# The slabs behind an inner norm run on the raw residual; the norm's mean and deviation are applied to their outputs

## The chip, the cores and the metric

The kernel runs on one core of a Trainium2 chip. The metric is the time of one execution on the device, in microseconds (us). The engines are TensorE (PE, with PEld for its weight loads), VectorE (DVE), ScalarE (ACT), GpSimd (POOL) and SyncE (SP, which only issues DMAs here).

## The reference, cut to what matters

Two layers work on 512 latent tokens and 256 context tokens of 1024 features. Layer 0 has attention, layer 1 gated linear attention (GLA); the second half of each layer is a gated ConvFFN. Every half ends in a residual sum and a layer norm, and the next half reads the normed stream, modulated by vectors that come from a conditioning vector:

```
def layer_norm(x, g, b):
    mu = mean(x); var = mean(square(x - mu))
    return (x - mu) * rsqrt(var + EPS) * g + b
sh1, sc1, g1, sh2, sc2, g2 = split(silu(cond) @ ada_w[i] + ada_b[i], 6)
a = h * (1 + sc1) + sh1
y = attn_mixer(a) if i % 2 == 0 else gla_mixer(a)
h = layer_norm(ALPHA * h + g1 * y, ln_g[i, 0], ln_b[i, 0])
u = (h * (1 + sc2) + sh2) @ w_up            # 1024 -> 5632
acc = conv_b + centred depthwise convolution of width 3 over tokens of u
f = (silu(gate half of acc) * value half of acc) @ w_down
h = layer_norm(ALPHA * h + g2 * f, ln_g[i, 1], ln_b[i, 1])
```

So there are four norms. Norm 0 stands between attention and FFN 0, norm 1 between FFN 0 and GLA, norm 2 between GLA and FFN 1 (512 tokens only, as norm 3), and norm 3 makes the output. The first three are the inner norms. Because a norm with modulation is linear in the tokens once mean and deviation are known, W·(gain·(h − mean)·rstd + shift) equals rstd·(W·(gain·h)) − mean·rstd·(W·gain) + W·shift.

## The kernel before

**Slabs.** The stream lies feature-major: `h_res` is 8 tiles (KT) of 128 features by 768 tokens (TOK) in fp32. Weights come as 185 slabs of 128x1024 fp32, each giving 128 output features from 8 input tiles. SP's queue loads them in order into four buffers (`slab_load`, L390); a load waits until the w_lo of four slabs before is made. ACT makes w_hi of a slab (L998, L1011), DVE w_lo = raw − w_hi (`rest`, L1452), and TensorE does for each k-tile hi·hi, hi·lo and lo·hi (`slab` L519 to L535, `slab_high_first` L514). ACT and DVE split slab s+2 while slab s runs. The outputs go to four PSUM tiles pm[0] to pm[3].

**Ada pairs.** The modulation vectors need 48 tiles of `ada_w`, loaded in pairs of 1 MB on the same SP queue (`ada_load`, L395), with `ada_taken` counting the pairs that DVE has reduced; the load of pair n waits for `ada_taken` n−1. DVE reduces a pair (`ada_pair`, four row sums L1476, L1478 and `take_pair` L1482 to L1486, which writes `mods`) in `beside`, behind two of the four slabs of an iteration of FFN 0. Ahead of the FFN 0 loop SP issues slab loads up to S_FFN0+7, `ada_load(22)`, and then the loop with the slab loads S_FFN0+8 and on.

**A norm.** While the last eight slabs before a norm come out, DVE adds the residual (L1657) and its sum over tiles (L1664), ACT squares, POOL adds the squares (`sums_phase`, L2069). `stats` (L600) then turns sums into means per token with matmuls that give 128x6 results, DVE's `norm_phase` (L1705) makes variance and reciprocal on 128x6 tiles, and two sets of matmuls (`spread`) spread mean and reciprocal over partitions into PSUM. DVE subtracts the mean (L1728) and multiplies by the reciprocal (L1734), each with one operand in PSUM. ACT's `modulate` (L1024) applies the fused gain and shift per tile (L1030) and makes x_hi (L1041), and x_lo comes from DVE for tiles 0, 3, 6 and from POOL for the other five (`low_part`, L2051). TensorE works on two slabs at once while the tiles arrive (`first_modulated`, L562 to L594) and then goes on with whole slabs. In GLA the first of them gives the gate's low-rank input, from which `logits` (L818) and `decays` (L1818) go in pairs between the next slabs. `fuse` (L1687) makes gain and shift from `mods`, `ln_g` and `ln_b`.

**FFN.** Up slabs come in groups of 8, 8 and 6 pairs, each followed by 8 down slabs. Of a pair, ACT makes the centre tap (L1170), DVE the two side taps and the product (L1779), and the result is split into hid_hi and hid_lo.

Of the kernel before, what the change touches and what calls it, by code (L numbers as in the profile page):

```python
# [59 lines left out]
PAIR_AFTER = (3, 4, 6, 7, 9, 10, 12, 13, 14)  # L60

# [14 lines left out]
class Order:  # L76
# [14 lines left out]
    def enter(self, i, per):  # L91
        self.extra, self.start, self.per = i * per, self.n, per

    def leave(self, count):
        assert self.n - self.start == self.per, (self.n - self.start, self.per)
        self.n, self.extra = self.start + self.per * count, 0


def trunk(nc, x_in, vec_in, rep_in, slabs_in, gates_in, first_in, ada_in, rope_in, band_in, eye_in, a2_in, level_in, out):
    ctx = ExitStack()  # L100
    with ctx:
# [34 lines left out]
        mean_w = place("mean_w", [1])  # L136
        ones = place("ones", [1])
# [7 lines left out]
        stat_a = place("stat_a", [2, 6])  # L145
# [29 lines left out]
        [mod_t], _ = scratch(free_at + 2 * 4 * TOK, ("mod_t", [4, TOK]))  # L175
# [3 lines left out]
        [gla_v, cum], _ = scratch(hid_at, ("gla_v", [TOK // P, 8 * P]), ("cum", [2, GLA_HEADS, TOK]))  # L179
# [16 lines left out]
        for b in range(3, GLA_LEVELS):  # L196
# [4 lines left out]
        [o_hi2], at = scratch(x_at, ("o_hi2", [KT, LAT]), dtype=FP32R)  # L201
        [pairs, o_g], at = scratch(at, ("pairs", [2, LAT]), ("o_g", [2, LAT]))
        assert at <= x_at + 4 * KT * TOK
        [faded], at = scratch(x_at + 4 * KT * TOK, ("faded", [4, LAT]))
        [o_lo2], at = scratch(at, ("o_lo2", [KT, LAT]), dtype=FP32R)
        assert at <= hid_at
# [12 lines left out]
                 "stat_done", "h_ready", "mod_f", "x_hi_done", "centred", "std_done", "lin_done", "silu_done",  # L219
# [5 lines left out]
                 "var_done", "std2", "less_mean", "mean_done", "rms_done", "spread", "r_done", "squared_h",  # L225
                 "x_sum", "gate_done", "gate_copied", "gate_open", "added", "sink_done", "low_v", "low_p", "ln_scaled", "stat_a", "mean_b", "stat_copied", "key_r"]
# [155 lines left out]
        def _(sp):  # L382
# [68 lines left out]
            with sp.Fori(2, 12) as i:  # L451
                for u in range(4):
                    slab_load(4 * i + u + S_FFN0, u)
                    if u % 2 == 1:
                        ada_load(2 * i + u // 2 + 19, 1 - u // 2)
            for i in range(12, 17):
                for u in range(4):
                    slab_load(4 * i + u + S_FFN0, u)
                    if u % 2 == 1 and 2 * i + u // 2 + 19 < ADA_TILES:
                        ada_load(2 * i + u // 2 + 19, 1 - u // 2)  # L460
# [40 lines left out]
        def _(pe):  # L501
# [60 lines left out]
            def first_modulated(base, c, tokens):  # L562

                lag = 2 if tokens == TOK else 3
                out_of = (lambda slot: pm[slot ^ base % 2]) if base != S_GLA else (lambda slot: pm[slot])
                pe.wait_ge(sem["split_lo"], base + 2)
                pe.wait_ge(sem["psum_free"], base)

                def high(slot, k):
                    for w in (w_hi, w_lo):  # L570
                        for at, a, b in pieces(tokens):
                            pe.matmul(out_of(slot)[:, at:at + b - a], w[slot][:, k * P:(k + 1) * P], x_hi[:, k, a:b],
                                      start=(k == 0 and w is w_hi), stop=False)

                def low(slot, k):
                    for at, a, b in pieces(tokens):
                        last = pe.matmul(out_of(slot)[:, at:at + b - a], w_hi[slot][:, k * P:(k + 1) * P], x_lo[:, k, a:b],
                                         start=False, stop=(k == KT - 1))
                    return last

                one, two = base % 2, (base + 1) % 2
                for k in range(KT):
                    slots = (one, two) if k < KT - lag else (one,)
                    pe.wait_ge(sem["x_hi_done"], KT * (c + 1) + k + 1)
                    for slot in slots:
                        high(slot, k)
                    pe.wait_ge(*low_of(c, k))
                    for slot in slots:
                        last = low(slot, k)
                last.then_inc(sem["slab_done"], 1)  # L590
                for k in range(KT - lag, KT):
                    high(two, k)
                    last = low(two, k)
# [1642 lines left out]
```

## Time and profile before

| | us |
|---|---|
| Median of three runs | 1715.65 |
| Lowest and highest | 1715.63, 1716.13 |
| Span of the profiled execution | 1712.9 |
| PE busy | 1651.3 (96%) |
| PEld busy | 1496.0 (87%) |
| DVE busy | 1103.4 (64%) |
| ACT busy | 711.4 (42%) |
| POOL busy | 100.0 (6%) |

The span is that of the profiled execution; the runs are timed from outside and lie some 2.75 us above it. The span holds 24053 instructions. In rows of the timeline the columns are the start in us, the duration, the engine, the line of the kernel, the operation with its output and inputs, and in brackets the idle time before it and what ended it. Consecutive equal instructions are drawn together as "xN" with one duration from the first's start to the last's end.

### The profile page before, as it was taken

Reading aid. Unit: us, or ns where it says so; the run is one execution under the profiler, and the core shown is the slowest. Engines: PE = TensorE matmul, PEld = TensorE weight load, DVE = VectorE, ACT = ScalarE, POOL = GpSimd, SP = SyncE. Lnnn points to the kernel's source line nnn. Section 1 sums busy time; section 2 is a strip of 40 time slices with the busy share of each in tenths; the row PEclk is TensorE's granted clock in tenths of the full one; section 3 lists DMA queues with packets and bytes.
Section 4 is the critical chain, followed back from the end, with each engine's and each line's share of the span. In section 5 each row is a group of like instructions: output and inputs, shape, how many; then the busy total and the mean of one; then the engine's idle time right before and its main releaser. Section 6 shows DMA issues by size and latency. Waiting matters only on the chain.

```text
span 1712.9 us, 24053 instructions
## 1 busy us (share of the span) xinstructions
PE 1651.3 (96%) x9008; PEld 1496.0 (87%) x9008; DVE 1103.4 (64%) x1796; ACT 711.4 (42%) x1104; POOL 100.0 (6%) x81
## 2 busy tenths in 40 slices
PE   8999999998999999999999899999989999999997
PEld 7999877898999999999999887977777788888885
DVE  6678666476888578865776555166645664464556
ACT  4222565336333233322334664255534543343345
POOL 0200000122000000000002200010002100000002
PEclk9999999999999999999999999999999999999999
DMA  9334100031434333343312022010123133333332
GB/s 362 129 136 161 49 1 1 25 136 38 139 107 147 135 111 130 115 142 141 111 61 89 27 74 62 24 36 26 38 62 98 62 98 98 99 98 99 92 92 74
DMA packets 37280, 159.51 MB, mean 93 GB/s; under 512 B 4145, under 2 KB 4401, under 8 KB 31057
## 3 DMA queue, kind: packets, MB, share of 16 engines
q1 hardware_dynamic: 37202, 158.44, 27.6%
q8 instruction: 52, 0.85, 0.2%
q14 instruction: 26, 0.21, 0.0%
HBM read 156.33 MB, written 2.10 MB: 92 GB/s over the span
## 4 chain that ended last, share of the span: by engine, by line
PE 87%; DVE 5%; ACT 5%; issue 2%; DMA 1%; POOL 0%; SPq 0%; ACTq 0%; DVEq 0%
PE pm L532 59%; PE pm L514 5%; PE pm L765 4%; PE pm L944 3%; PE pm L685 3%; PE pm L552 2%; PE pm L711 2%; PE pm L886 2%; PE pm L698 1%; ACT mod_t L1030 1%; PE pm L869 1%; DMA ada_w<-first_ada 1%; DVE h_res L1728 1%; PE pm L642 1%; PE pm L598 1%
## 5 line engine op out<-in xcount | busy, mean ns | idle before, releaser
L1452 DVE TENSOR_TENSOR w_lo<-raw,w_hi 128x1024 fp32r<-128x1024 f32 x185 | 231.0, 1250 | 341.5 <-ACT w_hi L1011 338.7
L1011 ACT ACTIVATE w_hi<-raw 128x1024 fp32r<-128x1024 f32 x181 | 191.7, 1059 | 601.6 <-PE pm L532 517.6
L532 PE MATMUL pm<-x_hi,w_hi 128*128 128x384 f32 (+1 forms) x1464 | 422.6, 349 | 1.1 <-DVE w_lo L1452 1.1
L532 PE MATMUL pm<-x_hi,w_lo 128*128 128x384 f32 (+1 forms) x1464 | 421.0, 348 | 0.0
L532 PE MATMUL pm<-x_lo,w_hi 128*128 128x384 f32 (+1 forms) x1464 | 421.0, 348 | 0.0
L532 PEld LDWEIGHTS pm<-x_hi,w_hi 128*128 128x128 f32 x1464 | 266.6, 188 | 16.9 <-issue 1.4
L532 PEld LDWEIGHTS pm<-x_hi,w_lo 128*128 128x128 f32 x1464 | 267.2, 188 | 14.2
L532 PEld LDWEIGHTS pm<-x_lo,w_hi 128*128 128x128 f32 x1464 | 267.3, 188 | 14.0
L1478 DVE CUSTOM_DVE_ANT_0 ada_w<-ada_w,cond_rep 128x1024 f32<-128x1024 f32 x80 | 102.6, 1283 | 0.0
L2069 POOL TENSOR_TENSOR sum<-sum,sq_t 128x768 f32<-128x768 f32 (+1 forms) x28 | 46.8, 1672 | 936.7 <-ACT sq_t L1140 936.7
L532 PE MATMUL pm<-hid_hi,w_hi 128*128 128x384 f32 (+1 forms) x330 | 98.8, 353 | 0.2 <-DVE w_lo L1452 0.2
L532 PE MATMUL pm<-hid_lo,w_hi 128*128 128x384 f32 (+1 forms) x330 | 98.7, 353 | 0.0
L532 PE MATMUL pm<-hid_hi,w_lo 128*128 128x384 f32 (+1 forms) x330 | 98.7, 353 | 0.0
L1196 ACT ACTIVATE hid_hi<-hid_f 128x768 f32 (+3 forms) x44 | 32.6, 742 | 131.0 <-DVE hid_f L1791 131.0
L1476 DVE CUSTOM_DVE_ANT_0 junk_f<-ada_w,cond_rep 128x1024 f32<-128x1024 f32 x56 | 68.3, 1220 | 0.0
L1794 DVE TENSOR_TENSOR hid_lo<-hid_f,hid_hi 128x512 f32 (+2 forms) x44 | 36.3, 826 | 44.7 <-ACT hid_hi L1196 44.7
L532 PEld LDWEIGHTS pm<-hid_hi,w_hi 128*128 128x128 f32 x330 | 60.4, 188 | 4.9 <-DVE w_lo L1452 0.7
L532 PEld LDWEIGHTS pm<-hid_hi,w_lo 128*128 128x128 f32 x330 | 60.3, 188 | 4.3
L532 PEld LDWEIGHTS pm<-hid_lo,w_hi 128*128 128x128 f32 x330 | 60.4, 188 | 4.2
L944 PE MATMUL pm<-x_sum,raw 128*128 128x512 f32 x128 | 59.2, 593 | 0.0
L685 PE MATMUL pm<-qkv 128*128 128x256 f32 (+3 forms) x176 | 55.3, 419 | 2.1 <-ACT probs_t L1077 1.3
L711 PE MATMUL pm<-probs_t,v_tok 128*128 128x128 f32 x400 | 54.0, 279 | 1.5 <-DVE x_lo L1587 0.7
(248 smaller groups left out, 2541.0 us busy)
## 6 DMA issues: line engine op xcount, KB each, us to landing
raw<-slabs SPq DMA_DIRECT2D x185, 512.0 KB, 3.6
ada_w<-ada SPq DMA_DIRECT2D x44, 1024.0 KB, 4.9
ada_w<-first_ada SPq DMA_DIRECT2D x4, 1024.0 KB, 18.3
raw<-gates SPq DMA_DIRECT2D x8, 512.0 KB, 3.5
h_res<-x SPq DMA_DIRECT2D x4, 768.0 KB, 16.3
out<-h_res SPq DMA_DIRECT2D x8, 256.0 KB, 2.0
rope<-rope SPq DMA_DIRECT2D x1, 512.0 KB, 22.9
level_f<-level SPq DMA_DIRECT2D x1, 448.0 KB, 3.2
```

The costliest lines, as they stand in the source:

```text
L514: last = pe.matmul(out_p[:, at:at + b - a], w[slot][:, k * P:(k + 1) * P], x[:, k, a:b], start=(k == 0 and w is w_hi and x is hi), stop=(k ...
L532: last = pe.matmul(out_p[:, at:at + b - a], w[slot][:, ks], x[:, k, a:b], start=(k == 0 and w is w_hi and x is hi), stop=(k == tiles - 1 a ...
L685: last = pe.matmul(pm[n % 3][:, at:at + b - a], q, qkv[:, u["k"], a:b], start=True, stop=(u["band"] is None or at > 0))
L711: last = pe.matmul(weighed(n), v_tok[:, t, u["v"] * P:(u["v"] + 1) * P], probs_t[:, n % 2, j * P:(j + 1) * P], start=(j == 0), stop=(j == ...
L765: last = pe.matmul(pm[j][:, at:at + b - a], w[slot][:, ks], x[:, k, a:b], start=(k == 0 and w is w_hi and x is hid_hi), stop=(k == tiles - ...
L944: last = pe.matmul(gate_bank, gate_raw(i)[:, k * P:(k + 1) * P], x_sum[k][:, :], start=(k == 0), stop=(k == KT - 1))
L1011: act.activation(w_hi[nxt % 2][:, :], raw[nxt % 4][:, :], ACT.Copy).then_inc(sem["split_hi"], 1)
L1452: dve.tensor_tensor(w_lo[nxt % 2][:, :], raw[nxt % 4][:, :], w_hi[nxt % 2][:, :].bitcast(FP32), ALU.subtract).then_inc(sem["split_lo"], 1)
L1476: junk_written = order.mark(dve.tensor_tensor_reduce(junk[:, :], w, cond_rep[:, 0, :], 1.0, 0.0, ALU.mult, ALU.add, to[:, half, 0:1]))
L1478: last = dve.tensor_tensor_reduce(w, w, cond_rep[:, 1, :], 1.0, 0.0, ALU.mult, ALU.add, to[:, half, 1:2])
L1794: dve.tensor_tensor(hid_lo[:, bass.ds(2 * i + u // 2, 1), 0:tokens].rearrange("p a b -> p (a b)"), hid_f[:, 0:tokens], hid_hi[:, bass.ds(2 ...
L2069: pool.tensor_tensor(sum2[:, 0:tokens], sum2[:, 0:tokens], sq_t[:, n % 2, 0:tokens], ALU.add).then_inc(sem["summed"], 1)
```

## The change

The first three slabs behind each inner norm become `raw_slabs`. Their input is the residual times the fused gain, split into hi and lo tile by tile while the residual is made (ACT `raw_hi`, DVE `raw_low`), so they need neither mean nor deviation. Two to four extra columns hold the gain and the shift vectors and give W·gain and W·shift. The statistics are four wide matmuls placed behind k-tile 3 of the first raw slab; mean, deviation and reciprocal are now 128x768 tiles in SBUF (`less`, `rstd`). Norming and modulating run beside the raw slabs for slab 3 (`paced_slab`) and all later ones. The raw outputs are finished in `take_raw` (DVE), a ScalarE `z` and a GpSimd `y`. POOL does seven of the eight low parts. ACT's splits of slabs +2, +3, +4 stand inside its modulating loop (SPLIT_AFTER), DVE's inside its scaling loop (REST_AFTER). The first iteration of FFN 0 has no ada pair any more, every later pair comes one iteration later, and the last group of up slabs has one more. GLA's logits follow other slabs. The last norm keeps its place and takes the wide statistics too. ATTN_OUT and GLA_OUT rotate over four banks.

```diff
+N_RAW = 3
+LOGITS_AFTER = {3: (0, 1), 4: (2, 3), 6: (4, 5), 8: (6, 7)}
-LOW_ON_VECTOR = (0, 3, 6)
+LOW_ON_VECTOR = (KT - 1,)
+SPLIT_AFTER = (0, 3, 6)
+REST_AFTER = (2, 5)
+PAIR_AT = [*range(12), *range(16, 20), *range(12, 16), *range(20, ADA_TILES)]
...
             ada_load(22, 0)
-            with sp.Fori(2, 12) as i:
+            for u in range(4):
+                slab_load(S_FFN0 + 8 + u, u)
+            with sp.Fori(3, 12) as i:
                 for u in range(4):
                     slab_load(4 * i + u + S_FFN0, u)
                     if u % 2 == 1:
-                        ada_load(2 * i + u // 2 + 19, 1 - u // 2)
+                        ada_load(2 * i + u // 2 + 17, 1 - u // 2)
...
+            def stats(c, tokens=TOK):                                   # PE
+                for at, a, b in pieces(tokens):
+                    last = pe.matmul(pm[2][:, at:at + b - a], less_w[:, 0:1].to_broadcast([P, P]), sum1[:, a:b], ...)
+                for at, a, b in pieces(tokens):
+                    last = pe.matmul(pm[3][:, at:at + b - a], mean_w[:, 0:1].to_broadcast([P, P]), sum2[:, a:b], ...)
+            def raw_slabs(c, tokens):
+                for u in range(N_RAW):
+                    pe.wait_ge(sem["split_lo"], base + u + 1)
+                    if u == 2:
+                        pe.wait_ge(sem["std2"], c + 1)
+                    for k in range(KT):
+                        if u == 0:
+                            pe.wait_ge(sem["raw_hi"], KT * c + k + 1)
+                            pe.wait_ge(sem["raw_lo"], KT * c + k + 1)
...
+                        if u == 0 and k == 3:
+                            stats(c, tokens)
+            def paced_slab(c, tokens, out_p):
+                pe.wait_ge(sem["split_lo"], s + 1)
+                pe.wait_ge(sem["psum_free"], s - 1 if c == 1 else s - 3)
...
+            raw_slabs(1, TOK)                                           # GLA
+            paced_slab(1, TOK, pm[1])
+            for u in range(N_RAW, 1 + 2 * GLA_HEADS):
+                if u > N_RAW:
+                    slab(S_GLA, 0, u, hid_hi, hid_lo, TOK if u <= GLA_HEADS else LAT)
+                for j in LOGITS_AFTER.get(u, ()):
+                    logits(j)
...
+                act.activation(tile_for(less), bank_of(pm[2], tokens), ACT.Copy)             # ACT norm_phase
+                act.activation(tile_for(rstd), bank_of(pm[2], tokens), ACT.Square)
+                act.activation(rstd[:, 0:tokens], rstd[:, 0:tokens], ACT.Sqrt, bias=col("eps"))
                 for n in range(KT):
                     act.wait_ge(sem["centred"], KT * c + n + 1)
                     modulate(n, c, tokens)
+                    if n in SPLIT_AFTER:
+                        u = SPLIT_AFTER.index(n)
+                        act.wait_ge(sem["slab_done"], base + u + 1)
+                        split(base + u + 2, base + u + 2)
...
+                dve.tensor_tensor(rstd, bank_of(pm[3], tokens), rstd, ALU.subtract)          # DVE norm_phase
+                def centre(n):
+                    dve.tensor_tensor(h_res[:, n, 0:tokens], h_res[:, n, 0:tokens], less[:, 0:tokens], ALU.add)
+                centre(0)
+                centre(1)
+                dve.wait_ge(sem["std2"], c + 1)
+                dve.reciprocal(rstd[:, 0:tokens], rstd[:, 0:tokens])
+                for n in range(KT):
+                    dve.tensor_tensor(h_res[:, n, 0:tokens], h_res[:, n, 0:tokens], rstd[:, 0:tokens], ALU.mult)
+                    if n + 2 < KT:
+                        centre(n + 2)
+                    if c < 3 and n in REST_AFTER:
+                        rest(base + 2 + REST_AFTER.index(n), ...)
+                take_raw(0)
+                take_raw(1)
+                rest(base + 4, base + 4)
...
+                take_raw(2)
+                rest(base + N_RAW + 2, base + N_RAW + 2)
...
-                        if layer == 0 and u % 2 == 1 and (g < 2 or (s0 == S_LAST_UP and i < 2)):
-                            ada_pair(20 + (s0 - S_FFN0) // 2 + u // 2 + 2 * i, ...)
+                        if layer == 0 and u % 2 == 1 and (g < 2 or (s0 == S_LAST_UP and i < 3)):
+                            ada_pair(18 + (s0 - S_FFN0) // 2 + u // 2 + 2 * i, ...)
...
-                        fuse(1)
+                        gain(1)
+                        fuse(1, tokens)
...
+                pool.tensor_tensor(less_r, less, rstd, ALU.mult)                             # POOL low_part
                 for n in LOW_ON_GPSIMD:
                     pool.tensor_tensor(lo[:, n, 0:tokens], mod_ring[n % 4], hi[:, n, 0:tokens], ALU.subtract)
+                for u in range(N_RAW):
+                    pool.wait_ge(sem["scaled"], N_RAW * c + u + 1)
+                    pool.wait_ge(sem["z_done"], N_RAW * c + u + 1)
+                    pool.tensor_tensor(to, raw_scaled(c, u)[:, 0:tokens], to, ALU.add).then_inc(sem["y_done"], 1)
```

## Rows read from the trace of the kernel before

**Rows 1.** The page, chain of work that ended last, share of the span by engine
```profile
PE 87%; DVE 5%; ACT 5%; issue 2%; DMA 1%; POOL 0%; SPq 0%; ACTq 0%; DVEq 0%
```

**Rows 2.** Windows: us, busy (x) PE, PEld, DVE, ACT, POOL, PEclk, DMA, GB/s
```profile
382.35:416.70 34.35, 28.82 (x170) 27.39 (x169) 20.70 (x28) 23.50 (x34) 9.89 (x6) 0.90 0.05 16
416.70:533.20 116.50, 116.50 (x674) 116.50 (x674) 99.98 (x182) 39.63 (x44) 0.00 (x0) 1.00 0.36 123
949.32:983.54 34.22, 28.97 (x170) 27.22 (x169) 21.56 (x30) 23.37 (x34) 9.19 (x5) 0.90 0.06 17
1319.76:1344.91 25.15, 20.16 (x97) 15.37 (x97) 15.41 (x28) 15.51 (x22) 6.88 (x6) 0.93 0.07 22
396.00:398.00 2.00, 2.00 (x8) 2.00 (x8) 1.88 (x3) 1.97 (x4) 0.00 (x0) 0.50 0.00 0
```

**Rows 3.** Timeline of PE in GLA: first logits, and values turned ahead of the third slab
```profile
983.54 2.84 PE L818 MATMUL pm<-low,a 32*128 32x512 f32 x8
...
1064.75 0.82 PE L838 MATMUL pm<-eye,v_turn 128*128 128x128 f32 x6
```

**Rows 4.** Groups by line and form: busy us, mean ns, idle before; DVE reciprocals
```profile
L1617 DVE RECIPROCAL row<-row 128x1 f32<-128x1 f32 x48 | 7.6, 159 | 0.8
...
L1723 DVE RECIPROCAL small<-small 128x6 f32<-128x6 f32 x2 | 0.4, 191 | 0.7 <-ACT small L1157 0.7
L1579 DVE RECIPROCAL head_r<-head_r 128x36 f32<-128x36 f32 x1 | 0.4, 368 | 0.0
```

**Rows 5.** Timeline of DVE and ACT behind norm 0
```profile
399.59 0.95 DVE L1734 TENSOR_TENSOR h_res<-h_res,pm 128x768 f32<-128x768 f32 x1
400.45 0.95 DVE L1728 TENSOR_TENSOR h_res<-h_res,pm 128x768 f32<-128x768 f32 x1
...
400.93 1.29 ACT L1030 ACTIVATE mod_t<-h_res,fused 128x512 f32<-128x512 f32 x2
...
403.01 1.30 ACT L1030 ACTIVATE mod_t<-h_res,fused 128x512 f32<-128x512 f32 x2
...
414.82 1.06 ACT L1011 ACTIVATE w_hi<-raw 128x1024 fp32r<-128x1024 f32 x1 [2.60 <-PE pm L577]
...
415.91 1.23 DVE L1452 TENSOR_TENSOR w_lo<-raw,w_hi 128x1024 fp32r<-128x1024 f32 x1 [4.79 <-ACT w_hi L1011]
...
426.45 1.22 DVE L1476 CUSTOM_DVE_ANT_0 junk_f<-ada_w,cond_rep 128x1024 f32<-128x1024 f32 x1
```

**Rows 6.** Timeline of POOL and DVE where both work at once
```profile
913.21 1.84 POOL L2069 TENSOR_TENSOR sum<-sum,sq_t 128x768 f32<-128x768 f32 x1 [498.43 <-ACT sq_t L1140]
914.05 2.09 DVE L1452 TENSOR_TENSOR w_lo<-raw,w_hi 128x1024 fp32r<-128x1024 f32 x1 [0.93 <-ACT w_hi L1011]
...
964.92 1.83 POOL L2051 TENSOR_TENSOR x_lo<-mod_t,x_hi 128x768 fp32r<-128x768 f32 x1 [15.75 <-ACT x_hi L1041]
965.48 0.95 DVE L1728 TENSOR_TENSOR h_res<-h_res,pm 128x768 f32<-128x768 f32 x1
...
1331.45 1.28 POOL L2051 TENSOR_TENSOR x_lo<-mod_t,x_hi 128x512 fp32r<-128x512 f32 x1 [11.85 <-ACT x_hi L1041]
```

**Rows 7.** DMA issues from 400 to 560: KB each, median us to landing
```profile
raw<-slabs SPq DMA_DIRECT2D x18, 512.0 KB, 4.0
ada_w<-ada SPq DMA_DIRECT2D x9, 1024.0 KB, 4.8
```

**Rows 8.** Waits of SP from 370 to 640: us in total, times, longest
```profile
SPq L395 <- DVE mods L1486: 123.1, 14, 10.4
```

**Rows 9.** Timeline of PE and DVE in the last norm
```profile
1694.94 2.02 PE L608 MATMUL pm<-mean_w,sum 128*128 128x128 f32 x16
...
1701.48 0.68 DVE L1734 TENSOR_TENSOR h_res<-h_res,pm 128x512 f32<-128x512 f32 x1
```

**Rows 10.** Timeline of PE, down slabs of the last group of FFN 0
```profile
911.74 0.51 PE L514 MATMUL pm<-hid_hi,w_hi 128*128 128x384 f32 x2
```

**Rows 11.** Timeline of PE, third slab of ATTN_OUT
```profile
332.35 0.59 PE L514 MATMUL pm<-x_hi,w_hi 128*128 128x384 f32 x2 [1.33 <-ACT tmp L1130]
```

More of the change, by code:

```diff
@@ L575, in low @@
[L575 removed]
+                            pe.matmul(out_p[:, at:at + b - a], w[s % 2][:, ks], hi[:, k, a:b], start=(k == 0 and w is w_hi),
+                                      stop=False)
+                    pe.wait_ge(*low_of(c, k))
                     for at, a, b in pieces(tokens):
[L577 to L579 removed]
@@ L581, in first_modulated @@
[L581 to L593, printed above, removed]
+                        last = pe.matmul(out_p[:, at:at + b - a], w_hi[s % 2][:, ks], lo[:, k, a:b], start=False,
+                                         stop=(k == KT - 1))
@@ L1141, in evacuate @@
                             sem["squared_h"], 1)
-                in_ffn = base not in (S_ATTN_OUT, S_GLA_OUT)
+                        if norm < 3:
+                            if n == 0:
+                                act.wait_ge(sem["gain_done"], norm + 1)
+                            for k, (a, b) in enumerate(kinds(tokens)):
+                                last = act.activation(RAW[norm][0][:, n, a:b], h_res[:, n, a:b], ACT.Copy,
+                                                      scale=fused[:, 0, n, k:k + 1])
+                            last.then_inc(sem["raw_hi"], 1)
                 if norm is not None:
@@ new lines, in ffn @@
+                    if g == 0:
+                        for u in range(4):
+                            evacuate(s0 + u, 0, u, raw_out(2 * layer, u) if u < N_RAW else pm[3], u if u < N_RAW else None)
+                            if u == 1:
+                                act.wait_ge(sem["slab_done"], s0 + 5)
+                                split(s0 + 6, s0 + 6)
+                        for u in range(4):
+                            step(s0, 1, u, evacuate, out=u, ahead=u > 0)
+                    with act.Fori(2 if g == 0 else 0, tiles // 2) as i:
+                        for u in range(4):
@@ new lines, in fuse @@
+                dve.wait_ge(sem["gain_done"], c + 1)
+                nk = len(kinds(tokens))
+                for o in range(2):
+                    at = tokens + nk * o
+                    hi, lo = (x[:, :, at:at + nk] for x in RAW[c])
+                    order.mark(dve.tensor_copy(hi, fused[:, o, :, 0:nk]))
+                    order.wait()
+                    last = dve.tensor_tensor(lo, fused[:, o, :, 0:nk], hi.bitcast(FP32), ALU.subtract)
+                last.then_inc(sem["extra_in"], 1)
@@ new lines, in ffn @@
+                    if g == 0:
+                        for u in range(4):
+                            evacuate(s0 + u, 0, u, raw_out(2 * layer, u) if u < N_RAW else pm[3], u if u < N_RAW else None)
+                            if u == 1:
+                                rest(s0 + 6, s0 + 6)
+                        for u in range(4):
+                            step(s0, 1, u, evacuate, out=u, ahead=u > 0)
+                            beside(1, u)
+                    start = 2 if g == 0 else 0
@@ new lines, in ffn @@
+                    with nullcontext(0) if unrolled else dve.Fori(start, tiles // 2) as i0:
+                        for i in range(tiles // 2) if unrolled else (i0,):
+                            if not unrolled:
+                                order.enter(i, 4 + per, start)
+                            for u in range(4):
+                                step(s0, i, u, evacuate, out=u)
+                                beside(i, u)
+                            if not unrolled:
+                                order.leave(tiles // 2 - start)
```

513 lines of the change are left out of this document (294 added, 219 removed).

## The prediction, as put on record

> **What bounds the kernel now.** I read the page first: its chain of work that ended last is PE for 87% of the span, with DVE and ACT at 5% each [rows 1]. So nearly all of the time is TensorE, and the change can win only where TensorE stands still or runs at a low clock. Cutting the span into windows around the inner norms shows where that is [rows 2]. From the first statistics matmul of norm 0 to the end of its two paced slabs TensorE is busy 28.82 of 34.35 us at a granted clock of 0.90, behind norm 1 28.97 of 34.22 us, behind norm 2 (512 tokens) 20.16 of 25.15 us. In the first of them the granted clock falls to 0.50, the lower of its two levels: 396 to 398 us, with TensorE busy throughout (last line). In the steady part TensorE is busy all 116.50 us: 14 slabs, so a slab of 768 tokens costs 8.32 us, one of 512 two thirds, 5.5. Two slabs would need 16.6 us where norm 0 takes 34.35: about 15 us a norm are the most that can be won. The steady part also shows DVE busy 99.98 of 116.50 us, 7.14 per slab of 8.32: whatever delays DVE is caught up slowly.
>
> Times below are us behind t0, the end of the last slab before the norm (382.35, 949.32, 1319.76).
>
> **Statistics and reciprocal, norm 0.** The new four statistics matmuls stream 1536 fp32 columns, as many as a pair of logits, which takes 2.84 [rows 3]. I take 2.8. Raw slab 0 starts near 0.8, gives four tiles (4.2), then the statistics: they end at 7.8. Slab 0 ends at 12.0, slab 1 at 20.4. DVE's subtraction and ACT's Sqrt, both 128x768 and about 0.9 to 1.3 each with their hand-over, bring the deviation to 11.0. Then comes a 128x768 reciprocal. The trace has it at 159 ns for 1 column, 191 for 6 and 368 for 36 [rows 4], 6.0 ns a column: 4.7 us, and 3.2 for 512 columns. Bounds: the 0.95 of a plain 128x768 tensor_tensor [rows 5] and, by the 6.4 ns a column between 1 and 6, 5.1. I take 4.7, since its own rows grow that way. The Trainium skill ("VectorE: DVE Perf Modes", First, the fixed hardware budget) says that a reciprocal repeats its divide steps 8 times; at that page's 0.96 GHz an estimate of 6.4 us, dearer than the rows say, by which the sum would be some 5.5 us higher.
>
> **Centring and scaling against GpSimd.** So the first centred and scaled tile is due at 15.7. Before, DVE's two operations a tile had one operand in PSUM and were issued every 0.86 [rows 5], with no loss beside a POOL operation: 0.95 at 965.48 while POOL ran from 964.92 to 966.75 [rows 6]. Afterwards `less` and `rstd` lie in SBUF, so both operands do. The one kind of DVE instruction with two SBUF operands that met POOL here is w_lo: 2.09 instead of 1.23 [rows 5, 6], for it starts at 914.05 and ends at 916.14, 1.09 behind the end of POOL's operation at 915.05. It stood still until POOL was done. The Trainium skill ("SBUF — State Buffer", Who interferes with whom) has that as a rule: a DVE instruction with two SBUF inputs and a GpSimd one that reads SBUF exclude each other for the whole instruction, one with a PSUM operand doesn't. Both rows agree with it. So I let every POOL operation of 1.84 (1.28 for 512 tokens, [rows 6]) insert itself whole into the DVE chain. POOL now has 7 low parts (5 before), `less_r` and 3 y's to do in just that stretch.
> Without exclusion: from 15.7 six DVE operations by 0.87 and the 1.23 of w_lo for slab 2 end at 22.1; six more and the next w_lo at 28.5; PE would do slabs 2 and 3 from 22.1 to 38.8. With it, 3 POOL operations come before the first w_lo (27.6) and 6 before the second (39.5): slab 2 runs 27.6 to 36.0, slab 3, which also follows its tiles, ends at 48.8. ACT at 2.08 a tile [rows 5] keeps ahead of that. Four slabs at 48.8 stand against 34.35+16.6=51.0 before: hardly anything won where 12 could be.
>
> **What is late next: an ada pair.** SP issues in order, and `ada_load(22)` stands ahead of slab loads S_FFN0+8 to 11; it waits for ada pair 20 (`ada_taken` 21). Before, DVE took that pair at once behind the norm, after the first up pair; now the first iteration has no pair and it is taken in i=1, behind the y's (50.7), the w_lo of slab 5 (53.6) and the evacuation of six slabs. Six slabs of DVE work are 6×7.14=42.8, less two pairs at 5.0 (four of 1.22 [rows 5] and their sums): 32.8, so 86.4. A pair's load lands 4.8 after its issue, a slab's 4.0 [rows 7]; slab base+8 queues behind the pair's, so between 4.0 and 8.8: I take 5.7, for both share the queues, and 0.4 for the issue. Then w_hi and w_lo take 2.3 [rows 5]: slab base+8 starts at 94.8, before at 34.35+6×8.32=84.3. **+10.5** (bounds: 0 if DVE is 10 us earlier, +13 if the load takes longest). SP waited for pairs 14 times in 370 to 640 us, up to 10.4 [rows 8]: hidden there because slabs were already in; here all four buffers behind it are empty.
>
> **Norm 1.** Same chain, but slab 3 needs bank 1, which comes free with `take_raw(1)`, behind all centring: start 44.3, end 52.7. The first logits were at 34.2 [rows 2, 3], now at 52.7; behind them one slab of 8.32 instead of three. Old stretch to the third value slab (983.54 to 1065.57 [rows 3]) 82.0, less 16.6, plus about 0.9 for decays with less cover: 119.0 against 116.3, **+2.7** (−10.0 without exclusion).
> **Norm 2**, by the same steps with 3.2, 0.6 to 0.7 a DVE operation and 1.28 a POOL operation: w_lo of slab 2 at 19.5, of slab 3 at 28.1, four slabs at 34.8 against 25.15+11.0=36.1; the raw evacuations then hold the next slabs by some 3: **+1.7** (−7.6 without exclusion).
> **Final norm**: nothing runs beside it, so all that is added is open: reciprocal 3.2 for 0.2, wide subtraction, Sqrt and copy, less the narrow spreads. Old first scaled tile 1701.48+0.68, 7.2 behind 1694.94 [rows 9]; new: 10.3 or so; the last is 0.7 later still because the first two centred tiles no longer run ahead: **+3.8** (bounds +1, +5).
> **Last group of FFN 0.** One ada pair more (i<3), `gain`, the fuse with its copies, before the down slabs: old w_lo ended at 916.14 [rows 6], +5.1 for the pair and 0.4: 921.6; PE wants it at 911.74+6.24 (six of eight k-tiles of 8.32) [rows 10], **+3.7** (bounds 0, +5).
> **Smaller parts.** ATTN_OUT with four banks takes away waits as the 1.33 in [rows 11]: **−1.3**. The raw low and high parts stand behind the down slabs: DVE has there two operations of 0.95 and a w_lo of 1.23 a slab [rows 5], some 1.3 more for the low part, and behind three of eight slabs of ATTN_OUT a pair of 5.0. Those come to 9.5 against 8.32, the next ones to 4.5, so they are made up: nothing (bound +2 at the last pair). The two to four extra columns of a raw slab and the swapped buffers move no slab: nothing.
> **Clock.** A stretch with idle of this kind had 0.90 over 34 us [rows 2], 3.4 us of full clock missing, about 2.5 of it while matmuls ran at 0.50. Two such starts come anew (slab base+8 behind 10 us idle, the slab 3 of norm 1 behind 9): **+5.0** (bounds 0, +8).
> Sum: 10.5+2.7+1.7+3.8+3.7−1.3+5.0=**+26.1**. Span 1712.9+26.1=1739.0; the median of the runs (1715.65) lies 2.75 above the profiled span, and what lies around the span does not change, so **1742**, A.
>
> **Rivals.** *B, the late load is hidden* (pair 20 taken 10 us sooner, or slab 8 landing early): −10.5 and one clock start −2.5: 1729. For it: DVE's pace was summed from averages. *E, the reciprocal costs like any wide operation* (0.95): 3.7 less at two norms of 768 and 2.3 at the other two, 12.0: 1730. Against it: three rows on one line. *C, the other side: no exclusion for centring and scaling*, because POOL gets only gaps, or the operations mostly miss each other: 0 in norm 0 (pair 20 taken by 76, just in time), −10.0, −7.6, +3.8, +3.7, −1.3, clock +2.5: −8.9, **1707**, faster. It decides as soon as the mean of a centring or scaling stays under 1.1 us while POOL works; 965.48 is for it, 914.05 against. *F, C and also the FFN 0 group and pair cost nothing*: 1697 or so (−8.9, −3.7, −2.5 and the rest from the final norm's bound). *G, exclusion for one POOL operation in four*: −8.9 and a quarter of the 35 between C and A, −0.1: no change, 1715.
>
> **Numbers.** A 0.42, B 0.14, E 0.06, C 0.19, F 0.06, G 0.07, and 0.06 for dearer ones (a reciprocal at the upper bound, later pairs late too: 1750). Within 0.2% (3.4 us, about what separates a change from none here) is G; faster C and F, 0.25; slower the rest, 0.68. The range 1700 to 1750 leaves out F, half of the dearer cases and the tails of the others, together 2 in 10. The likeliest own range is 1732 to 1750.
>
> **What would show it.** Mean of the centring and scaling operations 1.5 to 2 us or more in the first 25 us behind norms 0 and 1 (C: 0.9); reciprocals of 4.7 and 3.2; PE idle of 7 us ahead of slab 2 of norm 0, some 10 us ahead of S_FFN0+8, released by the DMA of raw; the first logits 18 us later behind norm 1; the tail from the last slab 22 us instead of 18. The forecast fails if DVE doesn't stand still beside POOL, or if pair 20 is taken in time.

## The result and the profile after

The changed kernel takes 1765.31 us (median of four runs, 1761.68 to 1768.71) against 1715.64 us: a ratio of 1.0283, 95% interval 1.0265 to 1.0301, so 2.8% slower (49.7 us). The forecast was 1742 with 1700 to 1750 as its range: the direction was right, the time lies 15 us above the range. The profiled execution has a span of 1765.7 us, 52.8 above that of before.

The page, chain of work that ended last, of the changed kernel:

```profile
PE 77%; DVE 15%; ACT 4%; issue 2%; DMA 1%; SPq 0%; ACTq 0%; DVEq 0%
```

Against [rows 1] ten points of the chain went from TensorE to VectorE. Windows of the changed kernel, columns as in [rows 2]: norm 0 from the end of the last slab to the end of slab 3, the start of slab S_FFN0+8, norm 1 in the same way, and norm 1 up to the third value slab:

```profile
386.50:438.27 51.77, 41.59 (x201) 39.35 (x202) 47.87 (x45) 30.39 (x44) 20.43 (x10) 0.87 0.14 47
482.88:488.40 5.52, 5.52 (x17) 5.52 (x18) 5.45 (x13) 2.15 (x3) 0.00 (x0) 0.50 0.49 153
978.83:1033.23 54.40, 41.79 (x202) 39.87 (x200) 45.37 (x36) 31.01 (x44) 23.60 (x11) 0.84 0.13 39
...
978.83:1104.13 125.30, 107.24 (x474) 91.94 (x472) 88.97 (x81) 73.99 (x93) 23.60 (x11) 0.88 0.14 42
```

Now four slabs lie in a stretch of 51.8 us, as four took before (51.0), and VectorE is busy 47.87 of them, POOL 20.43. The granted clock is 0.87 and 0.84 where [rows 2] had 0.90. Centring, scaling and reciprocal by form, VectorE of the changed kernel (busy us, mean ns, idle before):

```profile
L1857 DVE TENSOR_TENSOR h_res<-h_res,rstd 128x768 f32<-128x768 f32 x16 | 28.1, 1766 | 0.1
L1847 DVE TENSOR_TENSOR h_res<-h_res,less 128x768 f32<-128x768 f32 x16 | 18.3, 1153 | 0.0
...
L1853 DVE RECIPROCAL rstd<-rstd 128x768 f32<-128x768 f32 x2 | 9.9, 4944 | 0.0
L1853 DVE RECIPROCAL rstd<-rstd 128x512 f32<-128x512 f32 x2 | 6.7, 3347 | 0.0
```

The timeline of VectorE and POOL behind norm 0 shows where the 1766 ns come from:

```profile
406.21 2.62 POOL L2218 TENSOR_TENSOR less_r<-less,rstd 128x768 f32<-128x768 f32 x1 [17.43 <-DVE rstd L1853]
407.04 2.60 DVE L1847 TENSOR_TENSOR h_res<-h_res,less 128x768 f32<-128x768 f32 x1
409.56 2.59 DVE L1857 TENSOR_TENSOR h_res<-h_res,rstd 128x768 f32<-128x768 f32 x1
412.07 0.94 DVE L1847 TENSOR_TENSOR h_res<-h_res,less 128x768 f32<-128x768 f32 x1
...
414.68 2.83 DVE L1548 TENSOR_TENSOR w_lo<-raw,w_hi 128x1024 fp32r<-128x1024 f32 x1
```

An operation takes 0.94 alone and 2.6 when a POOL operation is in its way. TensorE's idle times, on its timeline (in brackets the wait and what ended it):

```profile
389.77 0.98 PE L659 MATMUL pm<-hid_hi,w_hi 128*128 128x384 f32 x2 [3.28 <-ACT tmp L1184]
417.57 1.01 PE L659 MATMUL pm<-hid_hi,w_hi 128*128 128x384 f32 x2 [6.75 <-DVE w_lo L1548]
482.88 1.00 PE L585 MATMUL pm<-x_hi,w_hi 128*128 128x384 f32 x2 [10.04 <-DVE w_lo L1548]
...
945.58 0.84 PE L585 MATMUL pm<-hid_hi,w_hi 128*128 128x384 f32 x2 [3.05 <-DVE w_lo L1548]
1005.17 1.01 PE L659 MATMUL pm<-x_hi,w_hi 128*128 128x384 f32 x2 [6.94 <-DVE w_lo L1548]
1022.02 0.98 PE L677 MATMUL pm<-hid_hi,w_hi 128*128 128x384 f32 x2 [5.67 <-issue]
```

The 10.04 us look like VectorE's, but w_lo waited for ACT and ACT for the transfer. SP, VectorE and ACT there:

```profile
474.00 0.16 DVE L1583 TENSOR_TENSOR mods<-ada_raw,vec 128x4 f32<-128x4 f32 x1
474.19 0.33 SPq L446 DMA_DIRECT2D ada_w<-ada  x1
474.56 8.73 SPq L441 DMA_DIRECT2D raw<-slabs  x5
...
480.43 1.06 ACT L1071 ACTIVATE w_hi<-raw 128x1024 fp32r<-128x1024 f32 x1 [12.04 <-DMA raw<-slabs]
```

Where the 52.8 us arose, in us, from starts of the same work in both timelines (before from [rows 2, 3, 9, 10], slab S_FFN0+8 worked out as in the prediction):

| | before | after | behind by | grown by |
|---|---|---|---|---|
| end of the last slab ahead of norm 0 | 382.35 | 386.50 | 4.2 | 4.2 |
| slab S_FFN0+8 starts | 466.6 | 482.88 | 16.3 | 12.1 |
| third down slab, last group of FFN 0 | 911.74 | 936.08 | 24.3 | 8.1 |
| end of the last slab ahead of norm 1 | 949.32 | 978.83 | 29.5 | 5.2 |
| values turned ahead of the third value slab | 1064.75 | 1104.13 | 39.4 | 9.9 |
| end of the last slab ahead of norm 2 | 1319.76 | 1359.86 | 40.1 | 0.7 |
| end of the last slab ahead of norm 3 | 1694.94 | 1744.04 | 49.1 | 9.0 |
| end of the span | 1712.9 | 1765.7 | 52.8 | 3.7 |

Two lines of the table hold time that no idle of TensorE explains: 8.1 us between S_FFN0+8 and the last down slabs (some 2.8 of them are the 5.52 us at half speed shown above), and most of the 9.0 between norms 2 and 3. Windows of equal length out of the middle of both FFNs show it, kernel before first:

```profile
600.00:740.00 140.00, 140.00 (x810) 140.00 (x809) 113.08 (x201) 46.07 (x52) 0.00 (x0) 1.00 0.37 124
1470.00:1600.00 130.00, 130.00 (x575) 107.69 (x575) 67.89 (x80) 49.59 (x64) 0.00 (x0) 1.00 0.31 95
```

and the changed one:

```profile
600.00:740.00 140.00, 140.00 (x799) 139.92 (x799) 104.27 (x182) 43.62 (x52) 0.00 (x0) 1.00 0.35 122
1470.00:1600.00 130.00, 130.00 (x562) 105.13 (x561) 65.92 (x77) 49.77 (x63) 0.00 (x0) 1.00 0.31 93
```

TensorE is busy all the time, at full clock, and still gets 799 matmuls done where it did 810, 562 where it did 575: 1.4% and 2.3% more for each plain matmul, in parts of the kernel where TensorE's work stands in the same order as before. The prediction has no term for that.

### The profile page after: what moved, and what is told of

Its sections match the earlier page's. It is cut to its first block, busy times and chain, and to the rows that moved or that the text cites. A ratio compares the mean times of both kernels' runs of the same rounds, so it can differ in the third digit from the quotient of the medians.

```text
span 1765.7 us, 23765 instructions
## 1 busy us (share of the span) xinstructions
PE 1666.3 (94%) x8868; PEld 1497.9 (85%) x8868; DVE 1194.0 (68%) x1845; ACT 745.8 (42%) x1162; POOL 141.4 (8%) x99
## 4 chain that ended last, share of the span: by engine, by line
PE 77%; DVE 15%; ACT 4%; issue 2%; DMA 1%; SPq 0%; ACTq 0%; DVEq 0%
PE pm L585 53%; PE pm L829 3%; PE pm L1005 3%; PE pm L750 2%; DVE w_lo L1548 2%; PE pm L606 2%; PE pm L567 2%; DVE h_res L1857 2%; PE pm L776 2%; PE pm L947 2%; DVE h_res L1847 1%; PE pm L763 1%; PE pm L930 1%; DVE rstd L1853 1%; DMA ada_w<-first_ada 1%
## 5 line engine op out<-in xcount | busy, mean ns | idle before, releaser
L585 PE MATMUL pm<-x_hi,w_hi 128*128 128x384 f32 (+1 forms) x1038 | 282.3, 345 | 11.4 <-DVE w_lo L1548 11.4
L585 PE MATMUL pm<-x_hi,w_lo 128*128 128x384 f32 (+1 forms) x1038 | 283.4, 346 | 0.0
L585 PE MATMUL pm<-x_lo,w_hi 128*128 128x384 f32 (+1 forms) x1038 | 282.2, 344 | 0.0
L585 PE MATMUL pm<-hid_hi,w_hi 128*128 128x384 f32 (+1 forms) x716 | 234.9, 369 | 4.8 <-DVE w_lo L1548 4.8
L585 PE MATMUL pm<-hid_hi,w_lo 128*128 128x384 f32 (+1 forms) x716 | 234.5, 369 | 0.0
L585 PE MATMUL pm<-hid_lo,w_hi 128*128 128x384 f32 (+1 forms) x716 | 234.4, 369 | 0.0
L585 PEld LDWEIGHTS pm<-x_hi,w_hi 128*128 128x128 f32 x1038 | 189.7, 189 | 17.9 <-issue 11.4
L585 PEld LDWEIGHTS pm<-x_lo,w_hi 128*128 128x128 f32 x1038 | 189.9, 189 | 4.8
L585 PEld LDWEIGHTS pm<-x_hi,w_lo 128*128 128x128 f32 x1038 | 189.8, 189 | 4.9
L585 PEld LDWEIGHTS pm<-hid_hi,w_lo 128*128 128x128 f32 x716 | 133.8, 190 | 15.8
```

Source lines behind the costliest of these rows:

```text
L585: last = pe.matmul(out_p[:, at:at + b - a], w[slot][:, ks], x[:, k, a:b], start=(k == 0 and w is w_hi and x is hi), stop=(k == tiles - 1 a ...
```

## The experiments

Theory: three losses on VectorE's and SP's queues that the prediction named (exclusion beside POOL, the late pair, the chain behind the reciprocal), and one that it missed: the four buffers of matmul operands now lie 772 columns apart instead of 768, because the raw slabs have four extra columns. Rival to the last: the new order or the smaller DMA scratch. Each kernel was timed beside the kernel before on the same chip; that one stood at 1716.35, 1716.49, 1715.49 and 1717.54 us in the four groups of runs.

**e1_stride_before**, on the kernel before:

```diff
-x_hi = place("x_hi", [KT, TOK], FP32R)          # x_lo, hid_hi, hid_lo alike
+x_hi = place("x_hi", [KT, TOK + 4], FP32R)
+... num_devices=1, dynamic_dma_scratch_size=1024)
```

> The kernel before with one thing of the change alone: x_hi, x_lo, hid_hi and hid_lo lie 772 columns apart instead of 768 (and the small DMA scratch of the changed kernel, which makes the room). Theory 'spacing': the plain slabs of the changed kernel are slow because their tiles start at odd places; a slab of 768 tokens goes from 8.32 to 8.42 us, one of 512 from 5.44 to 5.54, and over some 180 slabs the time grows by 12 to 16 us, to about 1729. Rival 'something else' (the new instruction order, the queues): slabs stay at 8.32 and the time within 3 us of 1715.6.

Measured 1733.19, ratio 1.0089 (1.0068 to 1.0110), a little more than the 12 to 16 expected, with the very counts of the changed kernel. The same two windows:

```profile
600.00:740.00 140.00, 140.00 (x799) 139.92 (x799) 108.60 (x192) 42.70 (x49) 0.00 (x0) 1.00 0.36 122
1470.00:1600.00 130.00, 130.00 (x562) 105.18 (x561) 67.33 (x80) 48.50 (x62) 0.00 (x0) 1.00 0.31 94
```

So 17 of the 50 us come without any raw slab.

**e5_scratch**, the small scratch alone on the kernel before.

> The kernel before with the small DMA scratch alone, tiles 768 columns apart: the other half of what e1_stride_before held. Theory 'spacing': nothing changes, 1716 within 3, slabs 8.32. Rival 'the scratch': 1733 as with both.

1715.60, ratio 0.9993 (0.9981 to 1.0006), 810 and 575 matmuls. It is the spacing.

**e2_pad16**: `TOK + 16` in place of `TOK + RAW_COLS` in the changed kernel's four buffers.

> The changed kernel with the four operand buffers 784 columns apart instead of 772, nothing else. Theory 'spacing': plain slabs are back at 8.32 and 5.44 us and the time falls by 12 to 16, to about 1751; the idle times behind the norms stay. Rival 'something else': 1765 within 4, slabs still 8.42.

1758.74, 6.6 us less: half a hit. 807 matmuls in the first window, but 563 in the second: at this spacing, a multiple of 64 bytes, the matmuls of 384 columns run nearly as before and those of 512 don't.

**e6_two_views**, the plain tiles 768 apart again:

```diff
+x_hi = place("x_hi", [KT, TOK], FP32R, at=top[0])
-x_hi = place("x_hi", [KT, TOK + RAW_COLS], FP32R)
+x_hi_r = place("x_hi_r", [KT, TOK + RAW_COLS], FP32R)   # and so on; RAW uses the _r views
```

> The changed kernel with two views of each operand buffer: the raw slabs read and write it 772 columns apart, everything else 768 apart as before. Theory 'spacing at 768': all plain slabs are back at 173.3 and 226.7 ns a matmul, 1765 falls by the 17 that e1_stride_before cost, to 1748. Rival 'only alignment to 64 bytes counts': no better than 784 columns gave, 1758.

1761.65, a miss of 13 us for my theory. Its groups by form in the window 1470 to 1600 tell why (busy us, mean ns; the kernel before has 389 for each):

```profile
L589 PE MATMUL pm<-hid_lo,w_hi 128*128 128x512 f32 x128 | 50.6, 395 | 0.0
L589 PE MATMUL pm<-hid_hi,w_hi 128*128 128x512 f32 x128 | 49.8, 389 | 0.0
L589 PE MATMUL pm<-hid_hi,w_lo 128*128 128x512 f32 x128 | 49.7, 388 | 0.0
L589 PE MATMUL pm<-x_lo,w_hi 128*128 128x512 f32 x40 | 15.8, 395 | 0.0
L589 PE MATMUL pm<-x_hi,w_hi 128*128 128x512 f32 x40 | 15.6, 389 | 0.0
```

Only the products with x_lo and hid_lo are slow. A buffer of 8x772 columns is 24704 bytes long, 128 more than a multiple of 256. Against the weights hid_lo has moved by 128 bytes, hid_hi by 256, x_lo by 384 and x_hi by 512; the slow ones are those where a remainder of 128 is left modulo 256. So the place seems to matter, modulo 256 bytes, and the next two runs test it.

**e9_even**: e6_two_views with `top[0] += 128` behind each of the four buffers.

> e6_two_views with 128 bytes put between the four operand buffers, so that each starts at the same place modulo 256 bytes as in the kernel before, relative to the weights too. In e6_two_views just the products with x_lo and hid_lo were slow, the buffers that had moved by 128 bytes. Theory 'place modulo 256': all plain matmuls are back at 173.3 and 226.7 ns, and 1761.7 falls by 12 to 14, to 1748. Rival 'the extra columns and views themselves cost': still 175.6, 1761.

1749.09, and the counts are those of before, 810 and 575:

```profile
600.00:740.00 140.00, 140.00 (x810) 140.00 (x809) 109.16 (x191) 44.13 (x53) 0.00 (x0) 1.00 0.36 124
1470.00:1600.00 130.00, 130.00 (x575) 107.67 (x574) 67.68 (x80) 50.04 (x64) 0.00 (x0) 1.00 0.31 97
```

**e12_weights**, on the kernel before: small scratch and `top[0] += 128` ahead of `raw_at`.

> The kernel before with the small DMA scratch and 128 bytes in front of the weight buffers (raw, w_hi, w_lo and all behind them), x and hid where they were. Theory 'relative place': what counts is where the moving operand lies against the weights, all three products are slow, 176 to 178 ns, and 1716 grows by 15 or more. Rival 'own place': only the address of the moving operand counts, 173.3 ns and 1716.

1738.49, ratio 1.0132 (1.0110 to 1.0154); 798 and 561 matmuls, all three products alike (394 to 395 ns each in the second window):

```profile
600.00:740.00 140.00, 140.00 (x798) 140.00 (x797) 108.37 (x190) 43.98 (x51) 0.00 (x0) 1.00 0.36 121
1470.00:1600.00 130.00, 130.00 (x561) 105.41 (x560) 66.23 (x78) 48.61 (x62) 0.00 (x0) 1.00 0.32 97
```

The moving operands lie where they were; the weights moved, and with them all that lies behind them. The matmuls of a plain slab read only moving operand and weights, so what fits all these runs is the place of one against the other.

**e3_ada_behind**:

```diff
-            ada_load(22, 0)
             for u in range(4):
                 slab_load(S_FFN0 + 8 + u, u)
+            ada_load(22, 0)
```

> The changed kernel with ada_load(22) behind the slab loads S_FFN0+8 to +11 instead of ahead of them. Theory 'late load': the 10.0 us of idle TensorE ahead of slab S_FFN0+8 go, and most of the half-speed stretch behind it (some 3 us more), so 1765 falls to about 1752. Rival 'VectorE is late anyway': the slab is there but its w_lo isn't made sooner, the idle time is then ended by w_lo instead of the DMA and at most 4 us are won, 1761 or more.

1757.18, 8 us less than the changed kernel, between the theory and its rival. The idle time ahead of the slab falls from 10.04 to 2.58:

```profile
474.54 0.61 PE L585 MATMUL pm<-x_hi,w_hi 128*128 128x384 f32 x2 [2.58 <-DVE w_lo L1548]
```

**e4_dve_lows**: `LOW_ON_VECTOR = tuple(range(KT))`; in the scaling loop VectorE makes low part n−3 behind scaling n, the last three behind `take_raw(1)`.

> The changed kernel with all eight low parts of a norm on VectorE, put between its own centring and scaling operations; GpSimd keeps less_r and the three sums y. Theory 'exclusion': a centring or scaling falls from 1.15 and 1.77 us to 0.95, though VectorE has seven operations of 0.95 more; slab 3 ends 8 to 10 us sooner behind norms 0 and 1 and 4 behind norm 2, in all about 1742. Rival 'work, not exclusion': VectorE's added work takes what GpSimd's gives back, 1760 to 1768.

1752.30, 13 us less (10 fewer than expected). The groups: scaling is back at 0.95, centring keeps the two operations that meet `less_r`.

```profile
L1846 DVE TENSOR_TENSOR h_res<-h_res,less 128x768 f32<-128x768 f32 x16 | 18.3, 1153 | 0.0
L1862 DVE TENSOR_TENSOR h_res<-h_res,rstd 128x768 f32<-128x768 f32 x16 | 15.1, 946 | 0.1
```

The wait for slab 2 halves (6.75 to 3.50, 6.94 to 3.71), though VectorE has seven operations more a norm. Less came out than expected because slab 3 ends only 3.1, 5.6 and 2.8 us sooner behind the three norms, where 8 to 10 and 4 were expected; VectorE now has the low parts itself. Behind norm 0 the late pair also keeps 7.05 us of idle time ahead of S_FFN0+8.

**e7_three** is e6_two_views, e3_ada_behind and e4_dve_lows together; **e10_even_three** has the 128 bytes too.

> Two views, ada_load(22) behind the four slabs, and all low parts on VectorE, together. If the three losses add up: 1765.3 less 17, 8 and 13, 1727. Rival 'they overlap' (the pair is late because VectorE is, so two of them win the same idle time): 1733 or more.

> e7_three with the same 128 bytes. Theory 'place modulo 256': 1743 less 13, 1730; the difference to 1716 is then what the norms themselves still lose (paced slabs, clock, the pair ahead of norm 1, the last norm). Rival: 1743.

1743.12 and 1729.70. e7_three missed because its spacing part was e6's, which wins 4 and not 17. Counting from 1761.65, the other two give 18.5 together, 8.1 and 13.0 by themselves: they nearly add up. e10_even_three came out as expected.

**e8_early**, and **e11_take** with the 128 bytes and `take_raw` in the loop (shortened; the comments are not in the kernel):

```diff
-SPLIT_AFTER = (0, 3, 6)
+SPLIT_AFTER = (-1, 2, 5)      # -1: ahead of the modulating loop
-REST_AFTER = (2, 5)
+REST_AFTER = (-1, 4)          # -1: right behind the reciprocal
+                    if c < 3 and n in (2, 3):      # e11_take; take_raw(1) into raw_h, not into less
+                        take_raw(n - 2)
```

> e7_three with the split of slab +2 ahead of the modulating loop and its w_lo right behind the reciprocal, slab +3's w_lo one tile sooner. Theory 'queue order': TensorE's idle time ahead of slab 2 (3.5, 3.7 and 3.8 us with the low parts on VectorE) goes and with it the half-speed stretch behind it, 4 to 5 us a norm, 12 to 15 in all below e7_three: about 1714. Rival 'only moved': the tiles come 1.2 us later, slab 3 waits instead for what slab 2 waited before, within 4 of e7_three.

> e10_even_three with e8_early's order and, so that bank 1 comes free early, take_raw(0) and take_raw(1) inside the scaling loop, take_raw(1) into a buffer of its own instead of less. Theory 'bank 1': the 9.9 us of idle time ahead of slab 3 behind norm 1 in e8_early fall to 3 or less, the other waits stay at 2, and 1730 falls by 8 to 16, to 1714 to 1722. Rival 'VectorE is full': what is taken early delays the tiles, and slab 3 waits for them, 1728 or more.

e8_early: 1744.24 against 1743.12, only moved. Slab 2 doesn't wait any more, but slab 3 of norm 1 does:

```profile
1000.80 0.98 PE L681 MATMUL pm<-hid_hi,w_hi 128*128 128x384 f32 x2 [9.94 <-issue]
```

The profile names no releaser; e11_take frees bank 1 early and that wait is 3.12. In time it won 4 us, 1725.71, between the theory (1714 to 1722) and its rival (1728 or more) and nearer the rival: the tiles stay late (2.90, 3.12 and 4.02 us ahead of slab 3 behind the three norms), as VectorE's chain is full.

**e13_lnexp**, on e11_take (shortened):

```diff
-act.activation(rstd, rstd, ACT.Sqrt, bias=col("eps"))
-dve.reciprocal(rstd, rstd)
+act.activation(rstd, rstd, ACT.Ln, bias=col("eps"))
+act.activation(rstd, rstd, ACT.Exp, scale=-0.5)      # VectorE centres four (six) tiles meanwhile
```

> e11_take without the wide reciprocal: the reciprocal deviation is exp(-0.5*ln(var+eps)) on ScalarE, and VectorE centres four tiles (six in the last norm) in that time instead of two. Theory 'the reciprocal holds VectorE's queue': VectorE is free 4.9 us sooner (3.3 with 512 tokens), the idle times of 2.9, 3.1 and 4.0 us ahead of slab 3 go and the last norm ends 3 us sooner, in all 8 to 12 us: 1714 to 1718. Rival 'the two table loads of ScalarE cost as much as they spare': within 4 of 1725.7.

1709.32, 16 us less (18 if each is taken against the kernel before in its own group), more than expected, and faster than the kernel before: ratio 0.9951 (0.9932 to 0.9969). ScalarE's row of it shows what replaced 4.94 us on VectorE:

```profile
397.15 0.94 ACT L1227 ACTIVATE rstd<-rstd,vec 128x768 f32<-128x768 f32 x1
398.10 1.28 ACT L1229 ACT_TABLE_LOAD   x1
399.40 0.85 ACT L1229 ACTIVATE rstd<-rstd 128x768 f32<-128x768 f32 x1
```

**e14_pairs**: the last six ada pairs at (i, u) = (0,1), (0,2), (0,3), (1,1), (1,3), (2,1) of the last up group, none right ahead of `gain(1)`.

> e13_lnexp with the last ada pair of FFN 0 taken out of the place right ahead of gain and fuse: the six pairs of the last up group stand behind slabs 1, 2, 3 of its first iteration, 1 and 3 of the second and 1 of the third. Theory 'one pair too many there': TensorE's 3.2 us of idle time in the down slabs and the half-speed stretch behind it go, 4 to 5 us less. Rival 'gain, fuse and the raw low parts are late by themselves': 1 us or less.

1704.45, 4.9 us less; the wait in the down slabs is gone. This is the best version, 0.9913 (0.9895 to 0.9931) of the kernel before. Window of norm 0 in it, from the end of the last slab to 1.1 us behind the end of slab 3:

```profile
383.31:427.30 43.99, 39.30 (x204) 37.00 (x204) 37.94 (x51) 33.91 (x48) 5.12 (x3) 0.96 0.17 58
```

The four slabs end at 426.17, so they take 42.9 us where the change had 51.8; VectorE is busy 37.94 and POOL 5.12 in the window.

**e15_start**: ada pairs of ATTN_OUT behind slabs 1, 3, 4 and `fuse(0)` behind slab 5.

> e14_pairs with ada pair 19 behind slab 4 of ATTN_OUT instead of slab 5, and fuse(0) behind slab 5 instead of 6. Theory 'the pair ahead of the last slab': the 3.65 us of idle time ahead of the first raw slab of norm 0 fall to 1 or less, 3 to 4 us less in all. Rival 'the residual chain of ScalarE and VectorE is that long anyway' (before the change it hid behind the statistics): 1 us or less.

1704.39: nothing won. The wait of 3.67 ahead of the first raw slab went (one of 1.54 came some slabs earlier) and slab +8 starts 1.6 us sooner, but the half-speed stretch of 3.4 us that followed that wait now follows the wait of 2.67 ahead of slab +8.

**e16_banks**: four banks in ATTN_OUT and GLA_OUT, on the kernel before.

> The kernel before with the four banks in ATTN_OUT and GLA_OUT alone. The prediction had 1.3 us less for it in ATTN_OUT: the two idle times of 1.33 and 1.36 us ahead of the third slab go, 1713 to 1714. Rival: what is won there is waited for again at the norm, 1716.

1715.96, ratio 0.9987 (0.9975 to 1.0000). In its trace the two idle times fall to 0.15 and 0.59 us, but in the time neither the −1.3 of the prediction nor nothing can be ruled out.

## Why the prediction was wrong

**The step that failed** is "The two to four extra columns of a raw slab and the swapped buffers move no slab: nothing." That term was put at nothing without a row behind it. The extra columns set the spacing of the buffers that every plain slab reads, and 1.4% and 2.3% on its matmuls is 17 us by e1_stride_before, 16 by e9_even against the changed kernel. 1742 and 17 are 1759, above the range. With the places put right and all else as changed, e9_even takes 1749.09, inside it. The same points as in the table above, in us by which each grew (the forecast's clock term of 5.0 halved between its two stretches):

| | forecast | changed | e9_even |
|---|---|---|---|
| end of the last slab ahead of norm 0 | −1.3 | 4.2 | 1.2 |
| slab S_FFN0+8 starts | 10.5 | 12.1 | 12.6 |
| third down slab, last group of FFN 0 | 2.5 | 8.1 | 1.5 |
| end of the last slab ahead of norm 1 | 3.7 | 5.2 | 5.1 |
| values turned ahead of the third value slab | 5.2 | 9.9 | 7.3 |
| end of the last slab ahead of norm 2 | 0 | 0.7 | 0.4 |
| end of the last slab ahead of norm 3 | 1.7 | 9.0 | 1.9 |
| end of the span | 3.8 | 3.7 | 3.7 |

Three of the starts in e9_even:

```profile
480.42 1.00 PE L593 MATMUL pm<-x_hi,w_hi 128*128 128x384 f32 x2 [10.10 <-DVE w_lo L1556]
927.01 0.51 PE L575 MATMUL pm<-hid_hi,w_hi 128*128 128x384 f32 x2
1092.43 0.82 PE L907 MATMUL pm<-eye,v_turn 128*128 128x128 f32 x6
```

So without the spacing every point of the forecast comes out within 2.5 us, and the sum 7.7 above it (33.8 for 26.1).

**Clock**: mis-sized, the second error. Two half-speed stretches were priced; in the changed kernel each of the waits shown above was followed by one, 5.52 us of TensorE at 0.50 behind the late pair alone. All stretches at 0.50 together, without the one at the end where TensorE has no work, six in the kernel before and twelve in the changed one (length, and busy time of each engine):

```profile
sum 27.30, PE 24.84 PEld 23.07 DVE 22.42 ACT 19.21 POOL 4.89; mean PE 4.14 PEld 3.85 DVE 3.74 ACT 3.20 POOL 0.81
sum 78.51, PE 54.93 PEld 50.32 DVE 57.64 ACT 42.41 POOL 21.10; mean PE 4.58 PEld 4.19 DVE 4.80 ACT 3.53 POOL 1.76
```

Half of TensorE's busy time there is lost, 12.4 and 27.5 us: 15 more, where the term had 5.0 and a bound of 8. That has the size of what the spacing leaves of the miss, but no run takes the clock away by itself.

**Exclusion**: right in kind. 0.94 alone, 2.6 beside POOL, 1.77 on average for scaling. The Trainium skill's rule ("SBUF — State Buffer", Who interferes with whom) agrees with these rows. w_lo of slab 2 ended 31.0 behind t0 (27.6 forecast) and slab 3 at 51.8 (48.8); raw slab 0 started 3.3 behind t0 where the forecast had 0.8, which is most of both differences. The w_lo was not the only such case in the kernel before: ahead of norm 0 a row sum of an ada pair took 2.85 instead of 1.22 beside POOL, which took longer as well.

```profile
370.12 2.80 POOL L2069 TENSOR_TENSOR sum<-sum,sq_t 128x768 f32<-128x768 f32 x1 [5.39 <-ACT sq_t L1140]
371.15 2.85 DVE L1478 CUSTOM_DVE_ANT_0 ada_w<-ada_w,cond_rep 128x1024 f32<-128x1024 f32 x1
```

**Reciprocal**: 4.94 and 3.35 for 4.7 and 3.2. Both lie between the two slopes read from the narrow rows (4.7 and 5.1 for 768 columns), a little nearer the upper one. The estimate from the Trainium skill ("VectorE: DVE Perf Modes", First, the fixed hardware budget), 6.4 us, is too high by the trace. The four take 16.6 us of VectorE together, and e13_lnexp, which takes them off VectorE and lets it centre meanwhile, won 16.

**The late pair**: right. Taken 87.7 behind t0 (86.4), the slab's w_hi starts 6.3 later (6.1), idle 10.04 (some 10); S_FFN0+8 starts 12.1 us later against t0, 10.5 forecast. Undone by itself it gives 8 us, since VectorE's w_lo still holds the slab for 2.58.

**Norm 1**: mis-sized. First logits at 54.3 (52.7), but the turned values grew by 9.9 instead of 2.7 and a clock term of 2.5. Between the logits there are two waits of about 2.5 us for VectorE's decays, where the forecast had 0.9 for less cover, and the granted clock from the end of the last slab to the turned values is 0.88 against 0.96. e9_even's 7.3 says that some 2.6 of the 9.9 are spacing.

**Last norm** 3.7 (3.8), **last group of FFN 0** a wait of 3.05 and 5.2 in all (3.7), of which e14_pairs wins 4.9: right. **Before norm 0** 4.2 instead of −1.3: that point differs by about 2 us between executions. e3_ada_behind and e4_dve_lows, with the changed kernel's instructions up to there, reach it at 384.3 and 384.1, and e5_scratch, with those of the kernel before, at 384.1 instead of 382.35. So neither the −1.3 nor the spacing can be read at that point.

**Open**: why a difference of place between operand and weights costs TensorE time. Of the place modulo 256 bytes only 0 and 128, and the mixed ones of 772 and 784 columns, were run.

## What to carry to other kernels

A few columns more at the end of a buffer can change the pace of everything that is read beside it: compare the count of matmuls in an untouched stretch of equal length before looking for idle time. Operations moved from 128x6 to 128x768 and from PSUM to SBUF operands cost twice here, by their length (a reciprocal of 4.94 us for 0.19) and by waiting for GpSimd (2.6 us for 0.95). And when a queue's work is moved later, look at the loads that stand in that queue behind it: here one line of SP's order was worth 8 us.

## What the runs showed of the hardware that was not expected

Plain fp32r matmuls with 384 and 512 moving columns go at 173 ns (140 us by 810) and 226 ns (130 by 575) each. With the moving operand shifted against the weights by 128 bytes modulo 256 they need 175.4 (798) and 231.7 (561), at full granted clock and with TensorE shown as busy throughout; moved by 256 bytes (hid_hi in e6_two_views) the busy time of a matmul is 388 to 389 ns as before, against 395. Moving the weights, and what lies behind them, by 128 bytes costs 23 us of 1715 (e12_weights).

A half-speed stretch that one wait no longer starts can be started by the next, smaller one: in e14_pairs 2.67 us of idle time ahead of slab +8 weren't followed by one, in e15_start, where the wait ahead of the first raw slab was gone, they were. The first 3.5 us of slab +8 in e14_pairs and in e15_start (granted clock 1.00 and 0.56):

```profile
463.97:467.40 3.43, 3.43 (x20) 3.43 (x21) 3.39 (x8) 0.85 (x1) 0.00 (x0) 1.00 0.83 311
462.38:466.00 3.62, 3.62 (x12) 3.62 (x13) 3.58 (x8) 0.84 (x1) 0.00 (x0) 0.56 0.86 324
```
